# Decoder trunk: the spreads of reciprocal roots contract over all 128 rows of TensorE, with zeros beyond their 8 or 16

## What is computed

```python
h = rmsnorm(x, g_mix[l]);  z = h @ w_in[l]
c_b, c_c, c_v, q, k, v, f_logit = jnp.split(z, SPLITS, axis=-1)
y_conv = short_gated_conv(c_b, c_c, c_v, conv_w[l])
y_conv = rmsnorm(y_conv.reshape(B, S, CONV_GROUPS, HEAD_DIM), ...)      # 8 groups of 64
q = rmsnorm(q.reshape(B, S, FOX_HEADS, HEAD_DIM), g_q[l])               # 8 heads of 64
k = rmsnorm(k.reshape(B, S, FOX_HEADS, HEAD_DIM), g_k[l])
y_fox = rmsnorm(forgetting_attention(q, k, v, log_f), ...)
x = x + jnp.concatenate([y_conv, y_fox], axis=-1) @ w_out[l]
x = x + mem_cross_attention(hx, m, w_xq[l], w_xkv[l], g_xq[l], g_xk[l]) @ w_xo[l]   # keys: rmsnorm of 4 heads of 128
x = x + swiglu(...)          # layer 0
x = x + moe_swiglu(...)      # layer 1: top 2 of 8 experts
```

## Time and profile before

| | |
|---|---|
| runs | 1392.94, 1401.37, 1408.19 us |
| profiled execution, its own time | 1404.88 us |
| span of its profile | 1403.4 us |
| mean granted TensorE clock | 0.984 of full speed |
| PE busy | 1367.6 us, 97% |
| DVE busy | 1031.5 us, 74% |
| ACT busy | 828.8 us, 59% |
| POOL busy | 77.1 us, 5% |
| read from HBM | 369.78 MB |

### The profile page before, as it was taken

How to read it: one execution, slowest core, us unless ns; L and a number is a source line. 1 busy time by engine, 2 the same in 40 slices (tenths; PEclk the granted TensorE clock), 3 DMA queues, 4 the chain that set the end, 5 groups by cost and what they waited for, 6 DMA issues and landing times.

```text
span 1403.4 us, 19621 instructions
## 1 busy us (share of the span) xinstructions
PE 1367.6 (97%) x7689; PEld 1197.1 (85%) x7689; DVE 1031.5 (74%) x805; ACT 828.8 (59%) x726; POOL 77.1 (5%) x84
## 2 busy tenths in 40 slices
PE   7999999999999999989999999999999999999998
PEld 6998889999889988878888888888888888888786
DVE  5548566554465485658888888978888888888887
ACT  5336355443354353537777767777677677676674
POOL 3100000000010000020000000000000000000400
PEclk9999899999999998989999999999999999999999
DMA  9523344564489223429999999999899899998994
GB/s 303 182 91 113 103 167 151 176 208 164 154 282 328 92 94 117 154 68 398 383 345 399 362 370 377 346 399 392 337 388 390 345 392 350 388 380 344 405 402 169
DMA packets 126628, 386.30 MB, mean 275 GB/s; under 512 B 7938, under 2 KB 61806, under 8 KB 126574
## 3 DMA queue, kind: packets, MB, share of 16 engines
q1 hardware_dynamic: 114686, 365.08, 69.6%
q0 software_dynamic: 3168, 11.54, 2.1%
q10 hardware_dynamic: 8720, 8.91, 1.8%
HBM read 369.78 MB, written 15.73 MB: 275 GB/s over the span
## 4 chain that ended last, share of the span: by engine, by line
PE 75%; DVE 8%; ACT 7%; DMA 6%; issue 3%; SPq 0%; ACTq 0%; DVEq 0%; POOL 0%
PE bank L1548 41%; PE bank L1544 16%; PE bank L1545 16%; DVE wl L1078 4%; DMA ring<-in_we_down 3%; DMA ring<-in_we_gate 3%; ACT wh L743 2%; DVE wl L1059 1%; ACT wh L729 1%; PE bank L2008 1%; DVE xl L1084 1%; ACT wh_third L743 1%; ACT xh L962 1%; ACT scratch L885 1%; ACT aT L759 1%
## 5 line engine op out<-in xcount | busy, mean ns | idle before, releaser
L1078 DVE TENSOR_TENSOR wl<-ring,wh 128x2816 fp32r<-128x2816 f32 (+1 forms) x127 | 400.2, 3170 | 61.2 <-PE bank L1548 36.4
L743 ACT ACTIVATE wh<-ring 128x2816 fp32r<-128x2816 f32 (+1 forms) x128 | 336.9, 2633 | 120.5 <-DMA ring<-in_we_down 45.4
L1059 DVE TENSOR_TENSOR wl<-ring,wh 128x3072 fp32r<-128x3072 f32 (+2 forms) x65 | 188.1, 2894 | 112.1 <-ACT wh L729 102.6
L1078 DVE TENSOR_TENSOR wl<-ring,wh_third 128x2816 fp32r<-128x2816 f32 (+1 forms) x64 | 187.0, 2923 | 28.6 <-PE bank L1548 22.4
L1544 PE MATMUL bank<-wh,xh 128*128 128x512 f32 x528 | 199.4, 378 | 8.2 <-DVE wl L1078 6.3
L729 ACT ACTIVATE wh<-ring 128x3072 fp32r<-128x3072 f32 (+1 forms) x64 | 151.4, 2366 | 80.2 <-PE bank L1545 43.5
L1545 PE MATMUL bank<-wh,xl 128*128 128x512 f32 x528 | 197.8, 375 | 0.0
L1548 PE MATMUL bank<-wl,xh 128*128 128x512 f32 (+1 forms) x768 | 194.8, 375 | 0.0
L743 ACT ACTIVATE wh_third<-ring 128x2816 fp32r<-128x2816 f32 (+1 forms) x64 | 155.6, 2431 | 46.3 <-DMA ring<-in_we_up 22.3
L1548 PEld LDWEIGHTS bank<-wl,xh 128*128 128x128 f32 x768 | 141.7, 188 | 18.4
L1544 PE MATMUL bank<-wh,ah 128*128 128x512 f32 x328 | 128.8, 393 | 1.7 <-DVE wl L1059 1.7
(11 more groups left out here) (273 smaller groups left out, 2055.9 us busy)
## 6 DMA issues: line engine op xcount, KB each, us to landing
ring<-in_we_gate SPq DMA_DIRECT2D x64, 1408.0 KB, 7.6
ring<-in_we_up SPq DMA_DIRECT2D x64, 1408.0 KB, 7.9
ring<-in_we_down SPq DMA_DIRECT2D x56, 1536.0 KB, 8.8
ring<-in_w_in SPq DMA_DIRECT2D x16, 1536.0 KB, 9.5
ring<-in_w_gate SPq DMA_DIRECT2D x6, 1536.0 KB, 6.5
ring<-in_w_up SPq DMA_DIRECT2D x6, 1536.0 KB, 6.6
ring<-in_w_down SPq DMA_DIRECT2D x6, 1536.0 KB, 6.5
rows_of<-zeros ACTq DMA_DIRECT2D x1, 8704.0 KB, 41.1
```

The costliest lines, as they stand in the source:

```text
L743: nc.scalar.activation(wh_in_pass(j, n), ring[:, slot, 0:n], ACT.Copy).then_inc(high_ready, 1)
L1059: nc.vector.tensor_tensor(wl[:, j, 0:n], ring[:, slot, 0:n], wh[:, j, 0:n].bitcast(F32), ALU.subtract).then_inc(low_ready, 1)
L1078: nc.vector.tensor_tensor(wl[:, j % 2, 0:n], ring[:, j % NSLOT, 0:n], wh_in_pass(j, n).bitcast(F32), ALU.subtract).then_inc(low_ready, 1)
```

## The change

The pattern `spreadg` and the three tensors of rows get 128 rows. The first 16 or 8 rows of the tensors keep their names, `mqk`, `mcv`, `mmk`, and are written as before. POOL clears the whole tensors once at the start. The pattern is made by the same memset and selects over 128 rows; beyond its 16 rows the selects leave zeros in all 1024 columns. The spreads pass 128 rows of both operands.

```diff
-        spreadg = sb("spreadg", [16, 8 * P])
+        spreadg = sb("spreadg", [P, 8 * P])
...
-        mqk = sb("mqk", [16, S])
-        mcv = sb("mcv", [8, S])
-        mmk = sb("mmk", [8, S])
+        mqk_rows = sb("mqk", [P, S])
+        mcv_rows = sb("mcv", [P, S])
+        mmk_rows = sb("mmk", [P, S])
+        mqk, mcv, mmk = mqk_rows[0:16, :], mcv_rows[0:8, :], mmk_rows[0:8, :]
...
             nc.gpsimd.tensor_copy(pick[:], pick32[:])
+            for rows_ in (mqk_rows, mcv_rows, mmk_rows):
+                nc.gpsimd.memset(rows_[:], 0.0)
             nc.gpsimd.memset(zeros[:], 0.0)
...
-                        spread_rows(l, "bq", spreadg[:], mqk[:], 8)
+                        spread_rows(l, "bq", spreadg, mqk_rows[:], 8)
...
-                spread_rows(l, "bc", spreadg[0:8, :], mcv[:], 4)
+                spread_rows(l, "bc", spreadg, mcv_rows[:], 4)
...
-                spread_rows(l, "bmk", spreadg[0:8, :], mmk[:], XH)
+                spread_rows(l, "bmk", spreadg, mmk_rows[:], XH)
```

More of the change, by code:

```diff
@@ L814, in _ @@
                 high_of(l, "z", 5)
-                guess_rows(l, "qk", "ssqk", mqk[:], 0.0)
+                guess_rows(l, "qk", "ssqk", mqk, 0.0)
                 for i in range(4):
@@ L853, in _ @@
                 square(l, "cv", zc[:, 4:8, :], zc[:, 0:4, :])
-                guess_rows(l, "cv", "ssc", mcv[:], 0.0)
-                guess_rows(l, "mk", "ssmk", mmk[:], epscol[0:8, :])
+                guess_rows(l, "cv", "ssc", mcv, 0.0)
+                guess_rows(l, "mk", "ssmk", mmk, epscol[0:8, :])
                 high_of(l, "wo", 0)
@@ L1167, in _ @@
                 low_of(l, "z", 4, 5)
-                refine_rows(l, "qk", "ssqk", mqk[:], 0.0)
+                refine_rows(l, "qk", "ssqk", mqk, 0.0)
                 low_of(l, "z", 6)
@@ L1228, in _ @@
                 then_wait(nc.vector.reciprocal(denom[:], denom[:]))
-                refine_rows(l, "cv", "ssc", mcv[:], 0.0)
-                refine_rows(l, "mk", "ssmk", mmk[:], EPS)
+                refine_rows(l, "cv", "ssc", mcv, 0.0)
+                refine_rows(l, "mk", "ssmk", mmk, EPS)
                 low_of(l, "wo", 0)
```

## The result

| | before | after |
|---|---|---|
| median of 12 runs | 1405.18 us (1392.94 to 1408.19) | 1388.18 us (1385.78 to 1391.22) |
| span of the profiled execution | 1403.4 us | 1386.4 us |
| mean granted clock | 0.984 | 0.995 |
| PE busy | 1367.6 us | 1351.1 us |

The ratio is 0.989, 95% interval 0.987 to 0.991. The profiled spans differ by 17.0 us, the medians by 17.0 us too. The prediction was 1385 us against a median of three runs, 1401.37, which the longer series puts at 1405.18; against its profiled execution it was 1388.5.

The account below looks back on a forecast made before the run. TensorE, busy 97% of the span, was taken as the bound, its clock halved behind spreads of few rows. Gains of 8.2 us per layer, 16.4 together, off the 1401.37 us median gave 1385 us; range 1376 to 1399.

Parts of the forecast that it names:

- (a): Products of all six spreads: 128 rows instead of 8 or 16 gain 0 to 0.8 us in all, taken as 0.
- (b): Stretch after `bq`, 3.4 us at half clock: full clock gains 1.5 us in each layer.
- (c): Head sums behind `bc`: 32 instructions at full clock gain 2.8 us in layer 0, 2.4 in layer 1.
- (d): The `bmk` spread: 3.78 us at half clock against 1.99 at full, gain 1.8 us in each layer.
- (e): First products of the output projection: full clock gains 2.1 us in layer 0, 2.5 in layer 1.
- all 16.4 us should reach the router: Way up to the router: waits move with TensorE, so the whole gain arrives and expert passes only start earlier.
- (f): POOL's start: three more memsets, 0.31 us each, ahead of `consts_ready`; bounds 0 and 0.9 us, taken as 0.
- (g): Router's stretch at half clock, begun 16 us sooner: may shorten or lengthen, bounded by 3 us each way, taken as 0.
- The chain of DVE, ACT and POOL: Head sums to `heads_transposed`: 8.6 us, stays hidden because TensorE's 11.2 us remain 2 us or more longer.
- rows do not matter: Spreads: the clock does not care for rows, so full rows change nothing, 1401 us; chance 13%.
- the head sums lower the clock: Behind `bc`: head sums lower it by themselves, so only 8.2 us gained, 1393 us, at worst 1398; chance 12%.
- The slower rival: Expert passes: an earlier start meets a slower feed and stretches every pass; 4.1 us a pass gives 1418 us; chance 5%.

Follow-up runs that it names:

- after_again: The changed kernel once more, no edit, for a second profile: 1389.8 us, ratio 0.9904 to the kernel before.
- rows64: The changed kernel with all six spreads over 64 rows instead of 128: 1391.17 us, ratio 0.9912 to the kernel before.
- dbl16: The changed kernel with every product of `bq` run twice in place, over 16 rows: 1406.63 us.
- dbl128: The changed kernel with every product of `bq` run twice in place, over 128 rows: 1397.44 us.
- before_b: The kernel before, unedited, profiled once more: one run, 1398.1 us.
- before_a: The kernel before, unedited, profiled once more: one run, 1407.1 us.
- bc_only: The kernel before with only the `bc` spread over 128 rows, `bq` over 16 and `bmk` over 8: 1397.52 us, ratio 0.9958.

## Why the prediction was right

Its steps, by starts of instructions (layer 0; layer 1 in brackets):

| step | predicted gain | measured |
|---|---|---|
| (a) form of the products, `bq` and `bc` | 0, at most 0.8 in all | 0.38 + 0.18 (0.37 + 0.19) |
| (b) behind `bq` up to `bc` | 1.5 (1.5) | 1.5 (1.5) |
| (c) head sums | 2.8 (2.4) | 2.7 (2.3) |
| (d) `bmk` | 1.8 (1.8) | 2.1 (2.1) |
| (e) projection up to the transposes | 2.1 (2.5) | 2.1 (2.45) |
| sum | 16.4 | 8.9 + 8.9 = 17.8 |

The mechanism, the places and the sizes of (b) to (e) held. The way to the router became 613.10 - 596.48 = 16.6 us shorter: 17.8, 0.3 from earlier starts of `bq`, less 1.5 for the fall at 558.5. That 1.5 is measured: from the transposes of layer 1 to the router it is 56.72 us against 55.19, and 55.26 in after_again, which lacks the fall. The prediction had no such term. All of the 16.6 us arrived at the end (17.0), as "all 16.4 us should reach the router" had it. The terms (f) and (g), put at 0, measured 0 and 0.3: from the router's first product to the first expert product it is 17.08 us instead of 17.40.

**Mis-sized:** step (a). It compared only how long eight products last (1.99 and 1.89) and took 0, with 0.8 us as the most. The runs show that few-row products among 128-row ones cost 0.2 to 0.4 us at each of six places, with rows64 against the kernel after as the clean case (0.19 in `bc`, 0.20 in the head sums behind it, 0.32 in `bmk`, of which 0.08 returns in the second product of the projection). In all 2.0 us instead of 0 (2 x 1.01, rows64 against the kernel after), above its upper bound. The Trainium skill (TensorEngine Tiling (Array Packing), Key Properties), which the prediction set beside it as nothing to the sum, says that a change of mode drains TensorE. The rows fit that, since the starts move apart at both ends of a spread, but no run shows a drain by itself. It was worth an eighth of the gain.

**The chain of DVE, ACT and POOL** stayed hidden, by 2.05 us where 2 or more was said.

**The rivals.** That rows do not matter is out by dbl16 against dbl128. The Trainium skill (TensorE: Matmul & The Clock Gate, What's actually happening) speaks of how busy the PE has been; the measurement decides against reading that as time without a gap: gapless 16-row products lost the clock in both layers of dbl16. That the head sums lower the clock is out by the 14 places where they stand between spreads of 64 or 128 rows and no fall follows. The slower rival placed the 15 us between the three runs in the feed of the expert passes, "which I can only place there". That step failed: before_b shows that most of its 7 us lies in how long the clock stays low behind the spreads, and after the change 12 runs spread over 5.4 us instead of 15.3. The passes do vary, 772.3 to 778.1 us over these profiles, by one wait in the last pass and the half clock beside it, which is the smaller part.

**The forecast's level.** It took the low stretches of one profile, 34 us, for those of the kernel. before_a has 34 too and before_b 20.5 there. Since the before median lies near the profiled execution (1404.88), the profile was a typical one; that was luck that one profile could not promise. Of the 3.2 us by which 1388.18 lies above the forecast of 1385, 3.8 are the base (a median of three runs, 1401.37, where twelve give 1405.18), and -0.6 is the gain, 17.0 instead of 16.4. The gain itself came so near because two errors nearly balance: (a) was too small by 2 us, and the fall at 558.5 took 1.5.

## What to carry to other kernels

When TensorE is busy without a gap and a stretch still runs at half the clock, look first at the rows of the operands just before it. In this kernel a contraction of 8 to 32 rows over 2 to 10 us put the dense products behind it at risk. Padding it with zeros to 128 cost nothing in TensorE's time, and gave back the 0.2 to 0.4 us that each group of few-row products cost besides. Judge such a change by a few profiles of each kernel, or by doubling the stretch, because in one execution the same instructions keep the clock and in the next they don't.

## What the runs showed of the hardware

- 128 rows with 8 columns keep the clock (4.0 us at 1.00, the first 0.5 us of them a product of 16 rows); 16 or 32 rows with 128 columns lost it in 8 of 12 places. Full rows are not enough everywhere: at the router's logits, 128 rows with 8 moving columns, the clock is lost in every profile. In six of the 14 it falls 0.5 to 3.1 us before their last product ends, so ahead of the wait behind them. What lowers it there is not shown.
- 64 rows kept it in all four places of rows64, one profile. They did not save the cost of the form: `bc` 1.92 us, as over 8 rows.
- Once low, the clock stayed low through 5.3 us of gapless head sums which at full clock do not lower it (3.5 us at 1.00 in bc_only and in the kernel after).
- The runs of one kernel differ mostly by its clock: 1393.71 us at 0.992, 1409.62 at 0.980, the same program.
